# Norm sums from VectorE, one tile for the beta and decay weights, real-token queries, regrouped tail additions

## The chip, the cores and the metric

The kernel runs on one core of a Trainium2 chip. Its engines run side by side: TensorE (PE in the rows; PEld is its weight load), VectorE (DVE), ScalarE (ACT), GpSimd (POOL) and SyncE (SP), whose queue starts the DMA transfers. The metric is the device time of one execution in microseconds (us), lower is better. The kernel before takes 1480.57 us (median of three runs, 1480.06 to 1481.06).

## The reference

Two transformer blocks, one after the other, on 512 tokens of width 1024, in float32. Cut to what the change touches:

```
def second_block(x, meta_tokens, w_in, ...):                 # after first_block
    h = concatenate([meta, x], axis=1)                       # 16 meta tokens + 512 real ones = 528
    u = rms_norm(h, norm_mix_pre)                            # norm 2 of the kernel: sum of squares over 1024
    proj = u @ w_in                                          # dq dk dv dz | db da | aq ak av
    beta = sigmoid(db); g = -exp(a_log) * softplus(da + dt_bias)     # 8 + 8 columns of w_in
    o_dn = gated_deltanet(dq, dk, dv) ; o_dn = rms_norm(o_dn) * silu(dz)
    q, k = rope(rms_norm(aq)), rope(rms_norm(ak))            # heads of 64
    o_at = softmax(q k^T) v
    h = h + rms_norm(concat(o_dn, o_at) @ w_out, norm_mix_post)      # norm 3
    u = rms_norm(h, norm_mlp_pre)                            # norm 4
    h = h + rms_norm(square(relu(u @ w_up)) @ w_down, norm_mlp_post) # norm 5, the last
    return h[:, 16:]                                         # the real tokens alone
```

The output leaves the meta tokens out, so the second block needs queries (`aq`) and the gate `dz` for real tokens only; keys, values and the recurrence need all 528. Norm 0 and norm 1 are those of the first block, whose SiLU feed-forward part ends right before norm 2.

## The kernel before, in words

Activations lie transposed: features on the 128 partitions, tokens along the row, so a width of 1024 is 8 tiles of 128 x 512 (or 528). Weights come as a stream of 204 units of 128 x 1024 (512 KB each). SyncE loads a unit into one of two `raw` buffers, GpSimd splits it into `w_hi` and `w_lo` (L467, L472) in one of four slots, and TensorE multiplies three products per tile of inner dimension (hi x hi, hi x lo, lo x hi): 24 matmuls of 512 columns for one unit. Where all 528 tokens are wanted, they are done in two halves of 264, 48 matmuls per unit. Semaphores order everything; each engine runs its own list in the order written. A split needs its slot free (`unit_done`) and its buffer loaded (`raw_ready`).

Units around the change: 88 to 109 are the down projection of the first block (the last two, 108 and 109, in `down_last`, tile by tile of the output, `f_done` after each), 110 and 111 keys and values (`tile_pair`, L1051), 112 to 115 the attention queries (`wide`, L1032), 116 to 131 the four parts of the recurrence (`wide_part`, L1374; the last four, `d` from 12, are `dz`), 132 to 139 the output projection, 140 to 203 the last feed-forward part.

A norm over features needs, for each token, the sum of squares over its 1024 values. ScalarE squares each of the 8 tiles into two alternating buffers (`n_sq`). Norms 0, 1, 3 and 4: VectorE adds the tiles into `n_rs` (`add_squares`, L1901) and one matmul with a matrix of ones sums over partitions (`sum_all`, L1078). Norms 2 and 5: a matmul with ones for each tile (`squares`, L1072), accumulating in PSUM; in norm 5 these stand between the tiles of `down_last`. These matmuls have float32 operands, and each shows as two rows. ScalarE then makes the inverse root with Ln and Exp (`root`), VectorE scales (`parts`: L1656 and L1642, both hi and lo of the next input).

The beta and decay columns (16 of them) are multiplied as three padded products of 128 columns (L1298), stored by ScalarE as rows (`bat`) and turned by five transposes (L1308).

For each tile of keys or queries the normal work is: ScalarE takes the squares and the scaled values out of PSUM (`k2_in`), a matmul sums over each head (`k2_side`, L1290), ScalarE makes the root (`k2_root`), VectorE rotates (L2030 to L2041).

The tail: VectorE scales the 8 tiles of the last norm (L2334) and adds the odd ones to `xT` (L2339), GpSimd adds the even ones (L546), SyncE writes each of the 8 tiles out (L445).

Of the kernel before, what the change touches and what calls it, by code (L numbers as in the profile page):

```python
# [139 lines left out]
def build(nc, w_stream, w_ba, x_t, vec, cst, cst1, cst2, pos, out):  # L140
    ctx = ExitStack()
    with ctx:
# [24 lines left out]
        AC = 23700  # L167
        arena = sb("arena", [P, AC])

# [114 lines left out]
        bat = n_h[0:16, 0, :]  # L284
# [4 lines left out]
        wba_hi, wba_lo = (g[:].rearrange("p a b -> p (a b)")[:, 0:KT * P].rearrange("p (a b) -> p a b", b=P) for g in (g_hi, g_lo))  # L289
# [89 lines left out]
        SUMMED = (0, 1, 3, 4)  # L379

# [28 lines left out]
        def _(sp):  # L409
# [40 lines left out]
        def _(pool):  # L450
            def split(i, held=False):
                for j in range(4):
                    if held and j == 3:
                        pool.wait_ge(S["h_ready"], parts_before(3))
# [21 lines left out]
            split(U_UP // 4, True)  # L476
            with pool.Fori(U_UP // 4 + 1, n0, 1) as i:
                split(i)
# [65 lines left out]
            for f in range(0, KT, 2):  # L544
# [5 lines left out]
        def _(act):  # L550
# [19 lines left out]
            def root(n, src, w):  # L570

                if n in SUMMED:
                    act.wait_ge(S["sum_done"], SUMMED.index(n) + 1)
# [176 lines left out]
            for j in range(2):  # L750
                act.wait_ge(unit_done[(us + j) % 4], ring_before(us, j, 5))
                a(g_hi[:, j, :], M1[:, 20 + j, :], ACT.Copy).then_inc(S["ms_hi"], 1)

# [3 lines left out]
            act.wait_ge(S["ba_loaded"], 16)  # L757
            act.wait_ge(S["ba_split"], 1)
            a(wba_hi[:, :, 0:16], wba32, ACT.Copy).then_inc(S["ba_split"], 1)

# [11 lines left out]
            def k2_in(t, n, u, gain):  # L772
# [3 lines left out]
                if t == 1:  # L776
                    act.wait_ge(S["ba_split"], 3)
                wait(act, S["k2_dve"], t - 1)
                a(flat(sq2[t % 2]), two(n), ACT.Square)
                a(flat(val2[t % 2]), two(n), ACT.Copy, scale=gain).then_inc(S["t2_read"], 1)  # L780

            def k2_root(t):
                act.wait_ge(S["k2_side"], t + 1)
                r = flat(root2[t % 2])
                inverse_root(ps[:, 4:6, 0:HALF], r, r, 1.0 / 64, vcol("eps"), S["k2_sqrt"])
# [5 lines left out]
            a(bat.rearrange("p (a b) -> p a b", a=2), ps[0:16, 4:6, 0:HALF], ACT.Copy).then_inc(S["bat_ready"], 1)  # L791
# [43 lines left out]
            def dn_copy(d):  # L835
# [4 lines left out]
                if d >= 12:  # L840

                    a(DZ[:, d - 12, 0:HALF - META], two(0)[:, 0, META:HALF], ACT.Copy)
# [788 lines left out]
        def _(dve):  # L1631
# [262 lines left out]
            def add_squares(n, f):  # L1894

                if f == 0:
                    return
# [503 lines left out]
```

## Time and profile before

| | before |
|---|---|
| median of 3 runs | 1480.57 us |
| profiled execution, time | 1483.68 us |
| profiled execution, span of the trace | 1481.6 us |
| mean granted TensorE clock | 0.977 of full speed |
| PE busy | 1388.2 us (94%) |
| DVE busy | 733.0 us (49%) |
| ACT busy | 430.8 us (29%) |
| POOL busy | 767.3 us (52%) |

The page profile shows one execution. Busy shares are over the whole span. The "chain" is the work followed back from the last instruction, at each step to what released it, so the time on it is time that the end waited for. Matmul rows overlap (one starts before the one ahead has drained), so the distance from start to start counts, not the duration. Windows give the granted clock as a share of 2.4 GHz: 1.00 is 2.4 GHz, 0.50 is 1.2 GHz.

### The profile page before, as it was taken

To read this page: it belongs to the slowest core of one execution; us is meant where nothing else is said; L and a number is where in the kernel's file an instruction comes from. 1 tells how busy PE (TensorE), PEld (TensorE's weight loads), DVE (VectorE), ACT (ScalarE), POOL (GpSimd) and SP (SyncE) were. 2 spreads that over 40 slices of the span, in tenths; PEclk is the share of its full clock that TensorE was granted. 3 is DMA by queue.
4 is the path that set the end of the run, shared out by engine and by line. 5 is a ranking of instruction groups with operands and counts; after the bars stand their busy time and mean duration, and the time that the engine had idled before them with its cause. 6 is when DMAs were issued, how large, how long until landed. Compare 5 with 4: busy or idle time off the path is not lost.

```text
span 1481.6 us, 20335 instructions
## 1 busy us (share of the span) xinstructions
PE 1388.2 (94%) x7550; PEld 1140.1 (77%) x7550; DVE 733.0 (49%) x1113; ACT 430.8 (29%) x842; POOL 767.3 (52%) x443
## 2 busy tenths in 40 slices
PE   7899999899999999999889999859989999999996
PEld 5677777687888887887888887639767888888884
DVE  6967766725544545113678885596534111211112
ACT  4254444413112112111344444334423111111111
POOL 5444533266666666765235432305255666676661
PEclk9999999999999999999999999978999999999998
DMA  5222211123222222222121111000022232233221
GB/s 190 86 85 71 86 57 62 53 87 114 95 92 97 99 99 86 99 99 86 44 71 43 53 49 53 20 1 2 29 86 71 99 99 93 91 100 99 99 71 57
DMA packets 31740, 113.87 MB, mean 77 GB/s; under 512 B 3520, under 2 KB 3904, under 8 KB 31424
## 3 DMA queue, kind: packets, MB, share of 16 engines
q1 hardware_dynamic: 31536, 112.85, 22.9%
q8 instruction: 42, 0.69, 0.2%
q10 hardware_dynamic: 144, 0.18, 0.0%
q14 instruction: 18, 0.15, 0.0%
HBM read 110.92 MB, written 2.10 MB: 76 GB/s over the span
## 4 chain that ended last, share of the span: by engine, by line
PE 83%; DVE 9%; ACT 4%; issue 2%; POOL 1%; DMA 1%; DVEq 0%; SPq 0%; ACTq 0%; POOLq 0%
PE ps L1032 40%; PE ps L1234 18%; PE ps L1374 6%; ACT arena L554 3%; PE ps L1051 3%; PE ps L1065 2%; PE ps L1254 1%; PE ps L1348 1%; PE ps L1072 1%; PE ps L1176 1%; PE ps L1328 1%; PE ps L1165 1%; PE ps L1137 1%; DVE arena L2166 1%; DVE arena L2171 1%
## 5 line engine op out<-in xcount | busy, mean ns | idle before, releaser
L472 POOL TENSOR_TENSOR w_lo<-raw,w_hi 128x1024 fp32r<-128x1024 f32 x204 | 515.1, 2526 | 66.6 <-ACT w_hi L554 50.9
L467 POOL TENSOR_SCALAR w_hi<-raw 128x1024 fp32r<-128x1024 f32 x188 | 202.4, 1076 | 544.1 <-PE ps L1032 184.9
L1032 PE MATMUL ps<-h_hi,w_hi 128*128 128x512 f32 (+1 forms) x976 | 377.3, 392 | 8.6 <-DVE arena L1685 5.2
L1032 PE MATMUL ps<-h_lo,w_hi 128*128 128x512 f32 (+1 forms) x976 | 370.1, 384 | 0.0
L1032 PE MATMUL ps<-h_hi,w_lo 128*128 128x512 f32 (+1 forms) x976 | 369.9, 384 | 0.0
L1032 PEld LDWEIGHTS ps<-h_hi,w_hi 128*128 128x128 f32 x976 | 182.3, 189 | 55.0 <-issue 10.6
L1032 PEld LDWEIGHTS ps<-h_lo,w_hi 128*128 128x128 f32 x976 | 182.4, 189 | 37.8 <-issue 2.5
L1032 PEld LDWEIGHTS ps<-h_hi,w_lo 128*128 128x128 f32 x976 | 182.3, 189 | 36.2
L554 ACT ACTIVATE arena<-ps 128x512 f32<-128x512 f32 (+7 forms) x205 | 96.5, 505 | 272.5 <-PE ps L1032 41.9
L554 ACT ACTIVATE arena<-arena 128x512 f32<-128x512 f32 (+6 forms) x191 | 101.5, 534 | 224.4 <-DVE arena L2319 134.2
L1234 PE MATMUL ps<-g_hi,w_hi 128*128 128x512 f32 x400 | 155.7, 389 | 0.9 <-DVE arena L1932 0.9
L1234 PE MATMUL ps<-g_hi,w_lo 128*128 128x512 f32 x400 | 155.6, 389 | 0.0
L1234 PE MATMUL ps<-g_lo,w_hi 128*128 128x512 f32 x400 | 155.6, 389 | 0.0
L1943 DVE TENSOR_TENSOR g_lo<-arena,g_hi 128x512 fp32r<-128x512 f32 x54 | 47.9, 896 | 212.9 <-ACT g_hi L554 212.9
L554 ACT ACTIVATE arena<-ps,V 128x512 f32<-128x512 f32 (+1 forms) x114 | 80.6, 725 | 195.8 <-DVE ps L1927 127.0
L554 ACT ACTIVATE g_hi<-arena 128x512 fp32r (+2 forms) x55 | 33.8, 625 | 219.0 <-PE ps L1234 218.3
L2319 DVE SCALAR_TENSOR_TENSOR arena<-ps,arena 128x512 f32<-128x512 f32 x32 | 21.8, 690 | 135.2 <-PE ps L1032 128.7
L1234 PEld LDWEIGHTS ps<-g_hi,w_hi 128*128 128x128 f32 x400 | 75.1, 188 | 17.0 <-DVE arena L1932 1.4
L1234 PEld LDWEIGHTS ps<-g_hi,w_lo 128*128 128x128 f32 x400 | 75.1, 188 | 15.6
L1234 PEld LDWEIGHTS ps<-g_lo,w_hi 128*128 128x128 f32 x400 | 75.1, 188 | 15.4
L2073 DVE SCALAR_TENSOR_TENSOR arena<-arena,V 128x528 f32<-128x528 f32 x48 | 62.3, 1298 | 18.1 <-ACT arena L554 16.8
L1927 DVE TENSOR_TENSOR ps<-ps,arena 128x512 f32<-128x512 f32 x33 | 23.1, 699 | 89.0 <-PE ps L1032 88.9
(283 smaller groups left out, 1863.5 us busy)
## 6 DMA issues: line engine op xcount, KB each, us to landing
raw<-in_w_stream SPq DMA_DIRECT2D x204, 512.0 KB, 3.5
xT<-in_x_t SPq DMA_DIRECT2D x2, 1056.0 KB, 7.2
out<-xT SPq DMA_DIRECT2D x8, 256.0 KB, 2.1
C<-in_cst SPq DMA_DIRECT2D x1, 576.0 KB, 10.1
arena<-in_cst SPq DMA_DIRECT2D x1, 528.0 KB, 4.3
arena<-in_pos SPq DMA_DIRECT2D x1, 256.0 KB, 3.9
V<-in_vec ACTq DMA_DIRECT2D x1, 174.5 KB, 5.9
band<-in_cst SPq DMA_DIRECT2D x1, 160.5 KB, 3.7
```

The lines of the kernel that those rows point to most:

```text
L467: pool.tensor_scalar(w_hi[j][:], raw[j % 2][:], 1.0, 1.0, ALU.mult, ALU.mult).then_inc(S["pool_step"], 1)
L472: pool.tensor_tensor(w_lo[j][:], raw[j % 2][:], w_hi[j][:], ALU.subtract).then_inc(split_done[j], 1)
L554: return nc.scalar.activation(o, i, f, **kw)
L1032: last = mm(dst[p], w[:, k, :], h[:, k, cols], start=(k == 0 and n == 0), stop=(k == KT - 1 and n == 2))
L1051: last = mm(dst[e][p], w[:, k, :], h[:, k, cols], start=(c == 0 and m == 0), stop=(c == KT - 1 and m == 2))
L1065: last = mm(ps[:, e, :], w[:, k, :], h[:, k, :], start=(k == 0 and m == 0), stop=(k == KT - 1 and m == 2))
L1234: last = mm(ps[:, f, :], w[:, f, :], h[:, j, :], start=(start and n == 0), stop=(stop and n == 2), skip_group_check=True)
L1374: last = mm(two(0)[c], w[u % 4][:, k, :], h[:, k, halves[c]], start=(k == 0 and n == 0), stop=(k == KT - 1 and n == 2))
L1927: v.tensor_tensor(ps[:, q + 1, :], ps[:, q + 1, :], n_ri[:, 0:T], ALU.mult).then_inc(S["up_scaled"], 1)
L1943: v.tensor_tensor(g_lo[:, j, :], src[:, ds(4 * i + j), :].rearrange("p a b -> p (a b)"), g_hi[:, j, :], ALU.subtract).then_inc(S["ms_ready ...
L2073: ins = v.scalar_tensor_tensor(out=y5, in0=x5[:, d % 2, j:j + L], scalar=vcol("dconv", 12 * j + d), in1=y5, op0=ALU.mult, op1=ALU.add)
L2319: v.scalar_tensor_tensor(out=rb[:, q, :], in0=ps[:, q, :], scalar=0.0, in1=n_ri[:, 0:T], op0=ALU.max, op1=ALU.mult).then_inc(S["relu_ready ...
```

## The change

- **Squares.** `squares` is gone. Every norm but the first is now summed in the same way: VectorE adds the squares of tiles 0 to 6 into `n_rs`, and `sum_all` multiplies ones with `n_rs` (waits for the seventh tile's addition) and then ones with the last square itself (waits for ScalarE alone), accumulating. Norm 2 has 4 such matmuls of 264 columns in place of 16, norm 5 two of 512 in place of eight and none between the tiles of `down_last`; norms 1, 3 and 4 have two of 512 in place of one, and one VectorE addition less. For norm 3 ScalarE squares the last tile before it copies it.
- **Around norm 2.** The preparation of masks and of the beta and decay weights stands ahead of the residual additions on VectorE. GpSimd does not begin unit 112 before the eight parts of norm 2's result are written (`held` at unit 112, `h_ready` 32).
- **Beta and decay.** hi and lo of the weights lie side by side in one tile (columns 0 to 15 and 32 to 47), multiplied with h_hi and h_lo: 32 matmuls in place of 48. The two groups of rows are added while they are turned: five float32 matmuls with a stationary operand of 48 rows and a selecting matrix of 16 columns, in place of five transposes.
- **Real tokens.** Units 112 to 115 and 128 to 131 are 24 matmuls of 512 columns in place of 48 of 264, with the work behind them (head sums, roots, rotation, copies) on 512 columns.
- **Tail.** VectorE scales all 8 tiles first and then adds tiles 4 to 7; GpSimd adds tiles 0 to 3.

```
-        wba_hi, wba_lo = (g[:]....[:, 0:KT * P].rearrange(...) for g in (g_hi, g_lo))
+        wba = arena_r[:, FT * T:FT * T + KT * P].rearrange("p (a b) -> p a b", b=P)
+        two_rows = band[0:48, 0:16]
...
             for f in range(KT):
-                if f % 2:
-                    sp.wait_ge(S["x_ready"], 24 + f // 2 + 1)
+                if f >= 4:
+                    sp.wait_ge(S["x_ready"], 24 + f - 3)
                 else:
-                    sp.wait_ge(S["x_pool"], f // 2 + 1)
+                    sp.wait_ge(S["x_pool"], f + 1)
                 sp.dma_start(out[:, f, :], xT[:, f, REAL]).then_inc(S["out_done"], 16)
...
-            with pool.Fori(U_UP // 4 + 1, n0, 1) as i:
+            with pool.Fori(U_UP // 4 + 1, U_DN2 // 4 - 1, 1) as i:
+                split(i)
+            split(U_DN2 // 4 - 1, 0)
+            with pool.Fori(U_DN2 // 4, n0, 1) as i:
                 split(i)
...
-            def squares(n, f, dst, cols):
-                pe.wait_ge(S["sq_ready"], 8 * n + f + 1)
+            def sum_all(n, dst, cols):
+
+                pe.wait_ge(S["sq_used"], 8 * n + 7)
                 for p, c in enumerate(cols):
-                    last = mm(dst[p], ones[:], n_sq[:, f % 2, c], start=(f == 0), stop=(f == KT - 1))
+                    mm(dst[p], ones[:], n_rs[:, c], start=True, stop=False)
+                pe.wait_ge(S["sq_ready"], 8 * n + 8)
+                for p, c in enumerate(cols):
+                    last = mm(dst[p], ones[:], n_sq[:, 1, c], start=False, stop=True)
                 last.then_inc(S["sq_used"], 1)
...
-                tile(u, 0, two(n), halves)
+                tile(u, 0, [ps[:, 2 * (n % 2), :]], [REAL])
...
-                for n, (w, h) in enumerate(((wba_hi, h_hi), (wba_hi, h_lo), (wba_lo, h_hi))):
+                for n, h in enumerate((h_hi, h_lo)):
...
-                last = nc.tensor.transpose(ps[:, 2, 16 * b:16 * b + 16], bat[:, c0:c0 + P], cst_ap("ident")[0:16, 0:16])
+                last = mm(ps[:, 2, 16 * b:16 * b + 16], bat[:, c0:c0 + P], two_rows, start=True, stop=True)
...
+            for n, name in enumerate(("ident", "neg_f", "neg_b")):
+                last = v.tensor_copy(masks[:, n, :], cst_ap(name))
+            last.then_inc(S["masks_ready"], 1)
+
+            dve.wait_ge(S["ba_loaded"], 16)
+            v.tensor_scalar(wba, cst_ap("ident").unsqueeze(1).to_broadcast([P, KT, P]), 0.0, None, ALU.mult).then_inc(S["ba_split"], 1)
             for f in range(KT):
                 dve.wait_ge(S["f_done"], f + 1)
                 v.tensor_tensor(xT[:, f, REAL], xT[:, f, REAL], ps[:, f, :], ALU.add).then_inc(S["x_ready"], 1)
...
+                if f:
+                    add_squares(2, f - 1, L)
...
             for f in range(KT):
                 scaled(f)
-                if f % 2:
-                    added(f)
+            for f in range(4, KT):
+                added(f)
```

How the order on the engines changes at three places. VectorE at the end of the first block, before (`f_done` rows are the residual additions):

```order
L1943 TENSOR_TENSOR g_lo<-arena,g_hi 128x512 [waits ms_hi] x2
L1960 TENSOR_TENSOR xT<-xT,ps 128x512 [waits f_done] x8
L1962 CAST masks<-C 128x128 x3
L1965 TENSOR_SCALAR g_hi<-C 128x1024
L1966 TENSOR_SCALAR g_lo<-C 128x1024
L1969 TENSOR_TENSOR g_lo<-arena,g_hi 128x8x16 [waits ba_split]
L1656 SCALAR_TENSOR_TENSOR arena<-xT,V,arena 128x528 [waits rs_ready]
```

and in the changed kernel, where L1903 adds squares and L1970 the residual:

```order
L1944 TENSOR_TENSOR g_lo<-arena,g_hi 128x512 [waits ms_hi] x2
L1960 CAST masks<-C 128x128 x3
L1964 TENSOR_SCALAR arena_r<-C 128x1024 [waits ba_loaded]
L1965 TENSOR_TENSOR band<-C 48x16
L1967 TENSOR_TENSOR arena_r<-arena,arena_r 128x8x16 [waits ba_split]
L1970 TENSOR_TENSOR xT<-xT,ps 128x512 [waits f_done] x3
L1903 TENSOR_TENSOR arena<-arena 128x528 [waits sq_ready]
L1970 TENSOR_TENSOR xT<-xT,ps 128x512 [waits f_done]
L1903 TENSOR_TENSOR arena<-arena 128x528 [waits sq_used,sq_ready]
L1970 TENSOR_TENSOR xT<-xT,ps 128x512 [waits f_done]
...
L1658 SCALAR_TENSOR_TENSOR arena<-xT,V,arena 128x528 [waits rs_ready]
```

The preparation moved ahead of the residual additions, one of the two 128x1024 fills is gone, and six additions of squares stand between and behind the residual additions. TensorE at the last matmuls of the program, before:

```order
L1254 MATMUL ps<-g_hi,w_lo 128x512
L1072 MATMUL ps<-arena,ones 128x512 [waits sq_ready]
L1072 MATMUL ps<-arena,ones 128x512 [waits f_done,sq_ready]
L1072 MATMUL ps<-arena,ones 128x512 [waits sq_ready] x2
L142 UNCONDITIONAL_BRANCH
```

and now:

```order
L1264 MATMUL ps<-g_hi,w_lo 128x512
L1084 MATMUL ps<-arena,ones 128x512 [waits f_done,sq_used,f2_ready]
L1087 MATMUL ps<-arena,ones 128x512 [waits sq_ready]
L142 UNCONDITIONAL_BRANCH
```

Behind the last product stand two matmuls with ones in place of four, and the four that stood further up between the tiles are gone too. VectorE in the tail, before:

```order
L2329 COPY arena<-ps 128x512 [waits sq_ready]
L2334 SCALAR_TENSOR_TENSOR arena<-arena,V 128x512 [waits rs_ready,f2_ready]
L2334 SCALAR_TENSOR_TENSOR arena<-ps,V,arena 128x512
L2339 TENSOR_TENSOR xT<-xT,arena 128x512 [waits f2_ready]
L2334 SCALAR_TENSOR_TENSOR arena<-ps,V,arena 128x512 x2
L2339 TENSOR_TENSOR xT<-xT,arena 128x512 [waits f2_ready]
```

and now:

```order
L2333 COPY arena<-ps 128x512 [waits sq_ready]
L1903 TENSOR_TENSOR arena<-arena 128x512 [waits sq_ready]
L1903 TENSOR_TENSOR arena<-arena 128x512 [waits sq_used,sq_ready] x5
L2340 SCALAR_TENSOR_TENSOR arena<-arena,V 128x512 [waits rs_ready,f2_ready]
L2340 SCALAR_TENSOR_TENSOR arena<-ps,V,arena 128x512 x7
L2345 TENSOR_TENSOR xT<-xT,arena 128x512 [waits f2_ready] x4
```

The additions to `xT` no longer stand between the scalings, and the additions of the squares stand ahead of them.

## Rows read from the trace of the kernel before

**Rows 1.** The page, chain that ended last, shares by engine.
```profile
PE 83%; DVE 9%; ACT 4%; issue 2%; POOL 1%; DMA 1%; DVEq 0%; SPq 0%; ACTq 0%; POOLq 0%
```
**Rows 2.** Chain in order of time, around norm 2: start us, us, what.
```profile
696.50 7.89 PE ps L1072 x32
...
704.41 0.71 ACT arena L554
...
708.15 13.44 PE ps L1051 x96
721.59 5.87 PE ps L1298 x48
...
729.36 0.41 PE ps L1308 x5
...
736.73 5.86 PE ps L1032 x48
```
**Rows 3.** Timeline of VectorE, end of the first block: start us, us, engine, line, work.
```profile
696.23 0.69 DVE L1960 TENSOR_TENSOR xT<-xT,ps 128x512 f32<-128x512 f32 x1 [0.67 <-PE ps L1254]
696.84 3.53 DVE L1962 CAST masks<-C 128x128 fp32r<-128x128 f32 x3
```
**Rows 4.** Windows of 1 us: length, PE, PEld, DVE, ACT, POOL busy (x), clock, DMA.
```profile
709.00:710.00 1.00, 1.00 (x8) 1.00 (x7) 0.96 (x2) 0.49 (x1) 0.00 (x0) 0.58 0.00 0
...
712.00:713.00 1.00, 1.00 (x8) 1.00 (x7) 0.96 (x3) 0.33 (x1) 0.00 (x0) 0.71 0.00 0
...
1108.00:1109.00 1.00, 1.00 (x5) 0.73 (x4) 1.00 (x3) 0.72 (x1) 0.00 (x0) 0.74 0.00 0
```
**Rows 5.** Chain at norm 1, norm 3 and norm 4.
```profile
345.89 0.86 PE ps L1078 x2
...
1096.87 1.09 ACT arena L554 x2
...
1097.99 0.70 DVE arena L1901
...
1098.73 1.14 PE ps L1078 x2
...
1104.96 23.71 PE ps L1065 x96
1128.67 0.88 PE ps L1078 x2
```
**Rows 6.** Timeline of TensorE: four float32 matmuls of 16 columns or so.
```profile
756.85 0.52 PE L1385 MATMUL ps<-arena,C 128*128 128x16 f32 x4
757.22 0.39 PE L1386 MATMUL ps<-arena,ones 128*128 128x32 f32 x2
```
**Rows 7.** Chain among the query tiles.
```profile
751.41 2.22 DVE arena L2031
...
757.91 2.80 DVE arena L2033
```
**Rows 8.** Timeline of GpSimd, same stretch.
```profile
757.41 2.72 POOL L472 TENSOR_TENSOR w_lo<-raw,w_hi 128x1024 fp32r<-128x1024 f32 x1
```
**Rows 9.** Chain, one of the `dz` units.
```profile
902.14 6.07 PE ps L1374 x48
```
**Rows 10.** Chain, last feed-forward part and last norm.
```profile
1449.19 5.45 PE ps L1254 x24
...
1463.63 3.61 PE ps L1072 x8
```
**Rows 11.** Timeline of the tail, ScalarE, VectorE and GpSimd.
```profile
1467.26 0.69 ACT L554 ACTIVATE arena<-ps,V 128x512 f32<-128x512 f32 x1 [1.22 <-PE ps L1072]
...
1468.72 0.75 DVE L2334 SCALAR_TENSOR_TENSOR arena<-arena,V 128x512 f32<-128x512 f32 x1 [16.82 <-ACT arena L554]
...
1471.29 1.40 DVE L2334 SCALAR_TENSOR_TENSOR arena<-ps,V,arena 128x512 f32<-128x512 f32 x2
...
1477.83 1.20 DVE L2339 TENSOR_TENSOR xT<-xT,arena 128x512 f32<-128x512 f32 x1
...
1469.56 1.26 POOL L546 TENSOR_TENSOR xT<-xT,arena 128x512 f32<-128x512 f32 x1 [27.25 <-DVE arena L2334]
```

More of the change, by code:

```diff
@@ L167, in build @@
         AC = 23700
+        with nc.sbuf_tensor("arena_r", [P, AC], F32R) as arena_r:
+            pass
         arena = sb("arena", [P, AC])
@@ L450, in _, with split @@
         def _(pool):
-            def split(i, held=False):
+            def split(i, held=None):
                 for j in range(4):
-                    if held and j == 3:
-                        pool.wait_ge(S["h_ready"], parts_before(3))
+                    if held == j:
+                        pool.wait_ge(S["h_ready"], parts_before(3) if j == 3 else parts_before(4))
                     pool.wait_ge(raw_ready[j % 2], 16 * (2 * i + j // 2 + 1))
@@ L543, in _ @@
                 split(i)
-            for f in range(0, KT, 2):
+            for f in range(4):
                 pool.wait_ge(S["f2_ready"], f + 2)
@@ L1243, in down4, with down_last @@
                 return body
-            def down_last(u0, j0, n, beside=None):
+            def down_last(u0, j0, n):
                 for e in range(2):
@@ L1267, in _ @@
             pe.wait_ge(S["x_ready"], 10)
-            for f in range(KT):
-                squares(2, f, [ps[:, 0, 0:HALF], ps[:, 1, 0:HALF]], halves)
+            sum_all(2, [ps[:, 0, 0:HALF], ps[:, 1, 0:HALF]], halves)
             pe.wait_ge(S["rs_ready"], 3)
@@ L1372, in wide_part @@
                     for n, (w, h) in enumerate(((w_hi, h_hi), (w_hi, h_lo), (w_lo, h_hi))):
-                        for c in range(2):
-                            last = mm(two(0)[c], w[u % 4][:, k, :], h[:, k, halves[c]], start=(k == 0 and n == 0),
-                                      stop=(k == KT - 1 and n == 2))
+                        for c, part in enumerate(halves if d < 12 else (REAL,)):
+                            last = mm(two(0)[c] if d < 12 else ps[:, 0, :], w[u % 4][:, k, :], h[:, k, part],
+                                      start=(k == 0 and n == 0), stop=(k == KT - 1 and n == 2))
                 if ks.stop == KT:
@@ L1617, in _ @@
                 down(U_DOWN2, FT, FT2 // 4 - 1, j, False, False)
-            def sum_beside(f):
-                if f == 3:
-                    pe.wait_ge(S["f2_ready"], 1)
-                if f >= 3:
-                    squares(5, f - 3, [ps[:, 0, :]], ALL)
-            down_last(U_DOWN2 + FT2 - 2, 2, FT + FT2, sum_beside)
-            for f in range(KT - 3, KT):
-                squares(5, f, [ps[:, 0, :]], ALL)
+            down_last(U_DOWN2 + FT2 - 2, 2, FT + FT2)
+            pe.wait_ge(S["f2_ready"], 1)
+            sum_all(5, [ps[:, 0, :]], ALL)
         @block.vector
```

94 lines of the change are left out of this document (46 added, 48 removed).

## Prediction

> **What bounds the kernel now.** I read the page first. The chain that ended last is TensorE for 83% of the span and VectorE for 9% [rows 1], so an edit counts where it takes matmuls out of TensorE's list or shortens a stretch in which TensorE waits. Then I read the chain in order of time at the six places that the change touches. At norm 1 and norm 4 it runs through the matmul with ones (0.86 and 0.88 us) [rows 5]. At norm 2 it runs through 7.89 us of matmuls with ones, then ScalarE's root, then the next pair of units, the beta and decay products, the five transposes and the query units [rows 2]. At norm 3 it goes ScalarE, VectorE's addition, the matmul, the root [rows 5]. The `dz` units are in it [rows 9], and so are the last norm and the tail [rows 10, 11]. All six are on the path; none lies behind a slack engine. The sum below is made against the profiled execution (1483.68 us, span 1481.6); the median shown is 3.1 us under it, and I take the same difference off both, since nothing here works on launch or end.
>
> **Norm 1 and norm 4: +1.7.** Each gets a second matmul with ones, behind the first, on the path. From start to start one is 0.86 us [rows 5]. The VectorE addition that goes was done long before TensorE arrived in both. 2 x 0.86 = +1.7. If the addition had been late the cost would be less, so the bounds are +1.0 and +1.8.
>
> **Norm 2: -4.9, and +0.4 for the clock.** The eighth residual addition starts at 696.23 and the next instruction of VectorE at 696.84 [rows 3]. In its place stands the addition of the seventh square, 0.70 us for one such addition [rows 5]; so `n_rs` is ready at about 697.6. The 32 rows of 7.89 us are 0.247 us each [rows 2]; four matmuls are 8 rows, 1.95 us. The last square (0.6 to 0.7 us for a ScalarE instruction of this width [rows 11], behind the residual addition that ends at 696.92) is ready before the second pair starts. The root then starts near 699.5 in place of 704.41 [rows 2]: -4.9. VectorE must keep pace in `down_last`: a tile takes 5.45/4 = 1.36 us [rows 10], a residual addition and an addition of squares take 0.61 + 0.70 = 1.31 as started back to back. It just fits, provided GpSimd is quiet; with GpSimd held before unit 112 it is, from about 689 on. Without that cover the casts show the price: 3.53 us for three small ones [rows 3] while GpSimd splits. The preparation that moved ahead has the 10.5 us in which VectorE now waits for the first finished tile; at the price seen (3.5 for the casts, about 3 for one fill) it ends some 3 us before that.
>
> The clock takes a little back. Before, TensorE worked until 704.4, waited until 708.15 and was granted 2.4 GHz until a little past 709, then 1.2 GHz until past 712 (0.58 and 0.71 in the mixed windows) [rows 4]: about 3.1 us at half clock, in a unit pair that TensorE bounds (13.44 us for 96 rows, where 48 pairs at 0.245 would be 11.7). Now TensorE idles sooner, from 696.2 with only 2 us of work in it, so the low clock is there from the first instruction, as it was behind norm 3, where work began at 1104.96 [rows 5] and 2.4 GHz came back in the window from 1108 (0.74) [rows 4], 3.5 us later or a little more. 0.5 to 0.8 us more at half speed costs 0.3 to 0.4.
>
> **Beta and decay: -1.4.** 48 matmuls in 5.87 us [rows 2] become 32: -1.95. Five transposes in 0.41 us [rows 2] become five float32 matmuls, two rows each. Four rows of such size take 757.22 - 756.85 = 0.37 [rows 6], so ten take 0.93: +0.5. Bounds +0.3 and +1.5, the upper if each row were as long as one with 264 columns divided by two.
>
> **Queries: -1.7.** A unit of 48 matmuls takes 5.86 us [rows 2], one of 24 matmuls of 512 columns 5.45 [rows 10]: -0.42 for a unit, four units. The first two are followed on the path by TensorE, and count in full. Behind the third the path runs through VectorE's rotation (2.22 and 2.80 us for instructions that take 0.7 alone) [rows 7]. These end when GpSimd's subtraction ends: the one of 2.72 us from 757.41 to 760.13 [rows 8] lies over the 2.80 us that end at 760.71. GpSimd starts when TensorE frees the slot, so it comes earlier by the same 0.42 and 0.84, and VectorE with it. So the last two count too, and I take -1.7; were they lost it would be -0.85, and with the narrower instructions on VectorE at most -2.1. The page "SBUF — State Buffer" of the Trainium skill, section "Who interferes with whom", says that a VectorE instruction with two SBUF inputs and a GpSimd instruction that reads SBUF exclude each other for the whole instruction; by that the third and fourth unit count in full, and rows 7 and 8 agree.
>
> What could spoil it is the hold. Units 112 and 113 are now split after norm 2's parts, from about 712.8, and with 114 and 115 GpSimd is busy without a break for 14 us, over the first rotation. TensorE wants unit 112 near 723, some 7 us after it is ready, and the rotated keys near 729, one or two us after I expect them. I cost it at nothing; if the cover fails, +1 to +3.
>
> **`dz` units: -1.75.** Same exchange, 6.07 us with the start [rows 9] less 0.42, four times, all on the path: -1.7, and one copy on ScalarE in place of two, -0.05. Bounds -1.0 and -2.1.
>
> **Norm 3: -1.0.** Before: two ScalarE instructions (1.09), the addition (0.70), the matmul, whose start to the root is 1.14 [rows 5]; the root starts 3.05 us after the last product. Now the matmul on `n_rs` starts at once (0.86), ScalarE squares first (0.60), and the second matmul ends 0.86 + 1.16 = 2.0 after the product: -1.0, bounds -0.8 and -1.3.
>
> **Norm 5: -4.95.** The last 48 products start at 1449.19 and take 2 x 5.45 = 10.9 [rows 10] without the four sums between them, so the last tile is finished at 1460.3. The seventh square (ready 1.36 before) is squared and added by 1460.2, so the two matmuls run at once: 0.86 + 1.16, root at 1462.3. Before it starts at 1467.26 [rows 11]. Bounds -4.2 and -5.1.
>
> **Tail: -1.8.** Before, from the first scaling at 1468.72 to the end of the last addition at 1479.03 is 10.3 us [rows 11]: 8 scalings at 0.68 and four additions of 1.20 that wait for GpSimd's 1.26. Now 8 scalings in 5.4 (they read PSUM and ran at 0.70 each beside GpSimd [rows 11]). GpSimd's four additions start 0.85 after the first and end 5.2 later, at 6.05; VectorE's first addition ends 0.55 behind that, three more take 0.63 each: 8.5. The output transfers follow 0.63 us apart; after the last one 2.6 us pass to the end of the span, as now. Bounds -0.9 (the transfers queue up) and -2.3.
>
> **Sum.** 1.7 - 4.9 + 0.4 - 1.4 - 1.7 - 1.75 - 1.0 - 4.95 - 1.8 = -15.4. Profiled execution 1468.3, median 1480.57 - 15.4 = **1465.2**.
>
> **Rivals.**
> - Two narrow matmuls cost only their share of columns. A pair of 264 costs 5.86/24 = 0.244 us and one of 512 costs 5.45/24 = 0.227 [rows 2, 10]; the gain of both groups of units, 3.4 us, rests on that 0.017, and the two figures come from different loops. If the pair cost 0.227 x 528/512 = 0.234 by itself and the rest were the loop's, 192 pairs would give 192 x 0.007 = 1.4 in place of 3.4: 1467.2. Against it: whole units, in the same run, at the same clock. Chance 0.1. "TensorE: Matmul & The Clock Gate" of the Trainium skill, section "Back-to-back issue gap", has a rule that leans the same way, N/2.4 + 2.5 ns from start to start: 225 ns for the pair, 216 for the wide one, an estimated 1.8 us for all. By that rule the sum would be -13.8; the rows are above it in both forms (244 and 227), more so in the narrow one.
> - Contention takes more: GpSimd's four splits in a row over the first rotation, or VectorE falling behind its 1.36 us for a tile in `down_last`. Place: 686 to 735. +2 to +5, time 1467 to 1470. For it: 2.22, 2.80 and 3.53 us for short instructions. Against: the hold covers norm 2, and the rotation has slack. Chance 0.17.
> - Slower than before: the hold starves TensorE. If after the hold each unit's split waited for its own load and for VectorE, and TensorE came to units 112 to 115 with none of them ready, four waits of 5 us or more would be needed to eat 15.4. The point is a split ready later than 723 + 5.45 per unit; GpSimd's larger half of a unit takes 2.72 us [rows 8], the whole some 3.5 to 4, and two raw buffers are full when the hold ends. Time 1482. Chance 0.02.
> - Norm 5 and the tail give less because ScalarE, VectorE and TensorE pass the last squares more slowly or the eight transfers bunch: -4.5 in place of -6.75, time 1467.4. Chance 0.1.
> - The forecast itself, within 1463.2 to 1467: 0.61.
>
> **How the numbers follow.** The forecast's own bounds, most ends taken at half, make 1463 to 1467. The contention case reaches to 1470; below, the clock or VectorE's overlap could give back 2 more. Range 1462.0 to 1469.5. A change of 0.2% is 3.0 us, about what a measurement tells from none. All cases but the third lie beyond it: faster 0.97, within 0.2% 0.015, slower 0.015.
>
> **What would show it.** Root of norm 2 about 3.5 us after the last residual addition begins (now 8.2); the unit pair behind it at low clock from its first row; 32 rows with the new weight tile near 3.9 us; query units 5.45 from start to start; norm 3's root 2.0 after its last product; norm 1 and 4 with two rows pairs of 0.86; last product to last root 2.0; first scaling to last addition 8.5. I am wrong if TensorE waits for `w_hi` at unit 112 or later, if residual additions in `down_last` drift behind `f_done`, or if VectorE's rotations are longer than before by more than 2 us in sum.

## The result, and the profile after

The changed kernel takes 1471.18 us in the median (1470.23 to 1473.29, 4 runs), the kernel before beside it 1480.82: ratio 0.9924, interval 0.9909 to 0.9939. It is 9.6 us faster; 15.4 were forecast, and 1471.18 lies outside the range.

Both profiled executions carry a part that has nothing to do with the change: no instruction differs ahead of the sum of norm 1, and yet the pair of units right ahead of that sum starts at 334.73 us before and at 331.57 after. Over all 17 profiles of this study that start lies between 331.57 and 338.22. So from here on I measure from the start of this pair, "from norm 1" for short, to the end of the span: 1481.60 - 334.73 = 1146.87 before, 1468.10 - 331.57 = 1136.53 after, a gain of 10.3 us.

The chain in order of time around norm 2 and the beta and decay products, after (start us, us, what), which answers [rows 2]:

```profile
694.51 0.71 DVE arena L1903
695.36 1.13 PE ps L1084 x4
696.49 0.90 PE ps L1087 x4
697.42 0.71 ACT arena L558
...
701.16 13.45 PE ps L1057 x96
714.61 3.92 PE ps L1306 x32
718.56 0.61 ACT arena L558
719.31 1.13 PE ps L1298 x4
720.44 1.21 PE ps L1316 x10
```

The 7.89 us of sums are 2.03 (L1084, L1087), behind the addition of the seventh square (0.71). The root (697.42) starts 3.5 us after the last product's end at 693.88, in place of 8.2. The pair of units is as long as before: 13.45 against 13.44, so the 0.4 that I gave the clock here did not fall due. The 48 beta products of 5.87 us are 32 of 3.92, but the ten rows that took the place of five transposes cost 1.21.

The chain at norm 3 and in the tail, after, which answers [rows 5, 10, 11]:

```profile
1089.93 0.86 PE ps L1084 x2
1090.79 0.97 PE ps L1087 x2
1091.78 0.70 ACT arena L558
...
1453.79 1.10 PE ps L1084 x2
1454.88 0.87 PE ps L1087 x2
1455.78 0.70 ACT arena L558
1456.50 0.64 ACT arena L558
1457.24 5.36 DVE arena L2340 x8
1462.60 0.95 DVE xT L2345
1463.56 0.60 DVEq L142
1464.16 1.21 DVE xT L2345 x2
```

The last norm runs two matmuls behind the last product, and eight scalings take 5.36 us before VectorE's additions: both as forecast.

What was not forecast shows in the windows. Columns are length, then PE, PEld, DVE, ACT and POOL busy (x instructions), granted clock (1.00 is 2.4 GHz, 0.50 is 1.2 GHz), DMA share, GB/s. The changed kernel at the start of the attention loop, at the first decay products, and late in the recurrence:

```profile
760.40:767.00 6.60, 5.21 (x24) 5.25 (x25) 5.08 (x9) 0.86 (x4) 0.95 (x1) 0.50 0.26 82
934.40:937.80 3.40, 3.40 (x7) 1.67 (x6) 0.00 (x0) 0.60 (x1) 2.49 (x5) 0.51 0.00 0
996.00:1002.50 6.50, 4.83 (x89) 4.64 (x89) 1.83 (x5) 2.15 (x5) 4.49 (x4) 0.50 0.01 3
```

The kernel before at the same two places, attention and first decay products:

```profile
770.60:774.00 3.40, 3.40 (x16) 3.40 (x17) 3.26 (x7) 0.77 (x2) 0.00 (x0) 0.50 0.43 159
943.22:947.00 3.78, 3.78 (x20) 2.73 (x21) 0.00 (x0) 1.20 (x2) 3.67 (x7) 1.00 0.02 4
```

At the attention loop half clock fills all 6.6 us of the window, which begins 1.4 us ahead of the loop (761.78 us), in place of 3.4 us from the loop's start (770.58). And it stands at the decay products, where in this execution of before it did not.

### The profile page after: what moved, and what is told of

Read it like the earlier page. It is cut to its first block, busy times and chain, and to the rows that moved or that the text cites. A ratio compares the mean times of both kernels' runs of the same rounds, so it can differ in the third digit from the quotient of the medians.

```text
span 1468.1 us, 19860 instructions
## 1 busy us (share of the span) xinstructions
PE 1373.4 (94%) x7309; PEld 1119.2 (76%) x7309; DVE 736.6 (50%) x1122; ACT 430.6 (29%) x838; POOL 768.2 (52%) x443
## 4 chain that ended last, share of the span: by engine, by line
PE 83%; DVE 10%; ACT 4%; issue 2%; POOL 1%; DMA 1%; DVEq 0%; SPq 0%; ACTq 0%; POOLq 0%
PE ps L1038 41%; PE ps L1244 18%; PE ps L1382 6%; ACT arena L558 3%; PE ps L1057 3%; PE ps L1071 2%; PE ps L1264 1%; DVE arena L2077 1%; PE ps L1356 1%; PE ps L1186 1%; PE ps L1336 1%; PE ps L1175 1%; PE ps L1147 1%; DVE arena L2175 1%; DVE arena L2170 1%
## 5 line engine op out<-in xcount | busy, mean ns | idle before, releaser
L1038 PE MATMUL ps<-h_hi,w_hi 128*128 128x512 f32 x944 | 376.4, 399 | 7.1 <-DVE arena L1687 4.3
L1038 PE MATMUL ps<-h_lo,w_hi 128*128 128x512 f32 x944 | 369.5, 391 | 0.0
L1038 PE MATMUL ps<-h_hi,w_lo 128*128 128x512 f32 x944 | 369.2, 391 | 0.0
L1038 PEld LDWEIGHTS ps<-h_hi,w_hi 128*128 128x128 f32 x944 | 178.2, 189 | 54.1 <-issue 10.4
L1038 PEld LDWEIGHTS ps<-h_lo,w_hi 128*128 128x128 f32 x944 | 178.1, 189 | 39.3 <-issue 2.9
L1038 PEld LDWEIGHTS ps<-h_hi,w_lo 128*128 128x128 f32 x944 | 178.3, 189 | 37.7
L558 ACT ACTIVATE arena<-ps 128x512 f32<-128x512 f32 (+6 forms) x201 | 96.4, 512 | 267.4 <-PE ps L1038 37.7
L558 ACT ACTIVATE g_hi<-arena 128x512 fp32r (+1 forms) x54 | 33.5, 630 | 218.3 <-PE ps L1244 218.3
L1244 PEld LDWEIGHTS ps<-g_hi,w_lo 128*128 128x128 f32 x400 | 75.1, 188 | 15.4
```

The costliest lines, as they stand in the source:

```text
L558: return nc.scalar.activation(o, i, f, **kw)
L1038: last = mm(dst[p], w[:, k, :], h[:, k, cols], start=(k == 0 and n == 0), stop=(k == KT - 1 and n == 2))
L1244: last = mm(ps[:, f, :], w[:, f, :], h[:, j, :], start=(start and n == 0), stop=(stop and n == 2), skip_group_check=True)
```

## The experiments

All stages below are read between the same instructions in each chain of waits: from their starts, or from the end of what released them. Each ratio is to the kernel before run in the same round. Its medians lay between 1480.82 and 1483.62 us, so kernels of different rounds are compared by their ratios. The first four kernels asked whether the missing time is clock or size.

**ctl_before and ctl_after**, both kernels unchanged.

> The kernel before, unchanged, for a second profile of it. Both theories expect 1480 to 1481 us. What it tells apart: in the first profile the stretch up to the first norm's last column took 3.16 us longer than in the profile of the changed kernel, though no instruction there differs. If that belongs to one execution, the second profile has this stretch 2 to 3 us shorter and the rest (norm 1 to the end) again at 1146.9 within 1 us; if it belongs to the kernel, it stays.

> The changed kernel, unchanged, for a second profile of it. Both theories expect 1470 to 1473 us. Theory A (the missing 4 to 5 us are lost where TensorE's clock is granted at half, and these stretches moved with the change: start of attention +0.8, start of the decay stage +1.7, recurrence +0.9): the second profile shows the low stretches at the same places of the program, the one at the start of the decay stage above all. Theory B (the terms of the queries, of the second wide stage and of the small fp32 matmuls were too large, and the low clock is scatter between executions): the low stretches lie elsewhere in this profile, and the time of the profiled execution moves by 1 to 3 us with them, while the stage of the queries gains 0.7 us again and not 1.7.

Medians 1482.99 (ratio to before 1.0005, 0.9993 to 1.0016) and 1471.78 (0.9921, 0.9901 to 0.9942). From norm 1 to the end the second profile of before has 1146.99 (1480.30 - 333.31), that of after 1136.76 (1470.20 - 333.44), within 0.12 and 0.23 of the first ones. So these executions differ ahead of norm 1, by up to 2 us, and their sums behind it agree; theory B's scatter of 1 to 3 us is not in them. But my sharpest piece of evidence moved: the second profile of before has half clock at the decay products too.

```profile
943.00:947.00 4.00, 4.00 (x16) 3.00 (x15) 0.00 (x0) 1.19 (x2) 2.86 (x5) 0.57 0.02 4
```

These products then take 1.7 us longer, and 1.4 of it came back later: from the first decay product to the end of the recurrence the two profiles of before have 105.54 and 105.85, the two of after 108.06 and 108.23. The stretch of decay and recurrence as a whole is 2.4 longer after, not its first products alone.

**one_sum**: norms 1 and 4 as before.

```
-                            sum_all(1, [ps[:, 7, :]], ALL)
+                            sum_one(1)
...
-                    sum_all(4, [ps[:, 7, :]], ALL)
+                    sum_one(4)
...
-                if f == 0 or f == KT - 1:
+                if f == 0 or (f == KT - 1 and n not in (1, 4)):
```

> The changed kernel with norms 1 and 4 as before: VectorE adds the last square and TensorE sums columns with one matmul, in place of two with the last square apart. The prediction's term for both is +1.7 us, and the two profiles agree at +0.86 each: so 1469.4 us, 1.7 below the changed kernel, by theory B. By theory A the saving can be lost or doubled by where the low stretches then fall: 1468 to 1471.

Median 1472.29 (ratio 0.9933, 0.9911 to 0.9954), no difference from the changed kernel that can be told. In the profile both terms are there: 368.75 against 369.59 between norms 1 and 2, 27.33 against 28.19 at norm 4. Then the pair behind norm 2 took 14.26 in place of 13.45:

```profile
700.48 14.26 PE ps L1057 x96
```

Half clock there lasted 6.8 us in this kernel and 3.4 in the changed one, and of the 1.7 us 1.0 is left from norm 1 to the end (1135.57 against 1136.53). That the shortening brought the 0.8 us at this pair is not shown: in narrow_z below, whose instructions up to here are those of the changed kernel, the pair took 14.42.

**keep_clock**: matmuls in TensorE's waits.

```
+            def fill(bank, w, x, count):
+                for _ in range(count):
+                    mm(ps[:, bank, :], w, x, start=True, stop=True)
...
+            fill_w(U_AT2, 5, 14)
...
+            fill(6, h_hi[:, 0, 0:P], h_hi[:, 1, 0:T], 14)
...
+            fill(6, h_hi[:, 0, 0:P], h_hi[:, 1, 0:T], 8)
...
+            fill_w(U_UP2, 5, 18)
...
+                    fill(6, h_hi5[:, 0, 0:P], h_hi5[:, 1, :], 8)
```

In this order they stand behind the sum of norm 2, ahead of the attention loop, behind its last sums, behind the sum of norm 3 and behind that of norm 4; `fill_w` waits for the unit's weights and calls `fill`.

> The changed kernel with filler matmuls of 128 by 512, whose results nobody reads, in five of TensorE's waits: 14 behind the sum of norm 2, 14 ahead of the loop of attention, 8 behind the last sum of the recurrence's norm, 18 behind the sum of norm 3, and 8 behind the sum of norm 4. Theory A: the granted clock stays at 1 across these waits, the wide stages behind them lose their slow first 3.4 to 6.8 us, and the kernel gains 3 to 7 us over the changed one (1464 to 1468). Theory B: filler does not reach the terms that were mis-sized; each filler that lasts longer than its wait costs what it sticks out (0.23 us a matmul), so 1471 to 1474.

Median 1463.26 (1461.14 to 1465.8), ratio 0.9867 (0.9841 to 0.9892): some 8 us below the changed kernel, a little more than the 3 to 7 of theory A. From norm 1 to the end 1127.85, 8.7 less. In its chain the pair behind norm 2 lasts 11.90:

```profile
703.74 11.90 PE ps L1057 x96
```

Its windows at the starts of that pair, of the attention loop and of the decay products have the full clock:

```profile
703.74:707.00 3.26, 3.26 (x27) 3.26 (x28) 3.19 (x5) 1.30 (x2) 0.00 (x0) 1.00 0.00 0
762.70:766.00 3.30, 3.28 (x27) 3.28 (x28) 3.12 (x8) 0.77 (x2) 0.00 (x0) 1.00 0.54 159
932.50:936.00 3.50, 3.49 (x17) 2.46 (x18) 0.00 (x0) 1.19 (x2) 3.38 (x7) 1.00 0.00 0
```

So half clock behind TensorE's waits costs this kernel 8.7 us, and it can be bought off with work that nobody reads. That alone doesn't say that it ate the change's gain; the same filler in the kernel before does.

**keep_before**: the kernel before with the same five lines.

> The kernel before with the same filler matmuls in the same five waits (their results are read by nobody). Filler took 8.6 us off the changed kernel, from the start of norm 1 to the end. Theory A (part of the gain that the prediction promised went into low-clock time that moved or grew: 0.8 at the start of attention, 2.35 in decay and recurrence, 0.5 at norms 3 and 4): filler takes less off the kernel before, 4 to 6 us, because it has less such time in these places, and changed minus before, both with filler, comes near -14. Theory B (the terms were mis-sized and the clock is the same burden on both): filler takes 8 to 9 off this one too, and the difference with filler stays at -10.3.

Median 1477.33, ratio 0.9954 (0.9937 to 0.9971). From norm 1 to the end 1141.42: filler takes 5.5 us off, not 8.7, as theory A had it. By stage (us; two profiles of before, two of after, then both with filler):

| stage | before | after | with filler | work | clock |
|---|---|---|---|---|---|
| pair at norm 1 to pair at norm 2 | 373.42, 373.41 | 369.59, 369.57 | 373.45, 369.59 | -3.86 | 0 |
| pair at norm 2 | 13.44, 13.45 | 13.45, 13.44 | 11.90, 11.90 | 0 | 0 |
| beta and decay | 8.18, 8.18 | 7.04, 7.03 | 8.18, 7.04 | -1.14 | 0 |
| two query units | 12.85, 12.87 | 12.27, 12.24 | 12.87, 12.24 | -0.63 | 0 |
| up to the attention loop | 27.96, 27.90 | 27.86, 27.86 | 27.88, 27.80 | -0.08 | 0 |
| attention loop | 172.64, 172.65 | 172.00, 172.08 | 171.09, 169.79 | -1.30 | +0.7 |
| decay and recurrence | 105.54, 105.85 | 108.06, 108.23 | 106.47, 106.94 | +0.47 | +2.0 |
| output units, norm 3 | 56.06, 56.05 | 55.04, 55.04 | 56.06, 55.10 | -0.96 | 0 |
| units behind norm 3, norm 4 | 26.82, 26.70 | 28.19, 28.21 | 25.17, 26.00 | +0.83 | +0.6 |
| last feed-forward, norm 5 | 335.60, 335.59 | 330.68, 330.70 | 333.99, 329.09 | -4.90 | 0 |
| tail | 14.36, 14.34 | 12.35, 12.36 | 14.36, 12.36 | -2.00 | 0 |
| sum | 1146.87, 1146.99 | 1136.53, 1136.76 | 1141.42, 1127.85 | -13.6 | +3.3 |

"Work" is the difference of the two kernels with filler, "clock" what the difference without filler adds to it (means of two).

At the attention loop and behind norm 3 filler took time off both kernels, 0.7 and 0.6 us more off the changed one. In all six profiles of kernels that start the loop as the changed one does, without filler, half clock there lasts 6.8 us; in all three that start it as the kernel before does (tail_only is the third), 3.4. In decay and recurrence it is otherwise: filler took 1.2 off the changed kernel (108.15 to 106.94) and added 0.8 to the kernel before (105.70 to 106.47). So "clock" in that row is a difference in where half clock fell, not a price that filler took off.

**tail_only**: the kernel before with norm 5's squares on VectorE and the new tail.

```
-            down_last(U_DOWN2 + FT2 - 2, 2, FT + FT2, sum_beside)
-            for f in range(KT - 3, KT):
-                squares(5, f, [ps[:, 0, :]], ALL)
+            down_last(U_DOWN2 + FT2 - 2, 2, FT + FT2)
+            pe.wait_ge(S["f2_ready"], 1)
+            sum_two(5, ps[:, 0, :])
...
```

> The kernel before with only the last norm's squares summed on VectorE and the tail regrouped. The prediction's terms -4.95 and -1.8: 6.75 below the kernel before, and every stage ahead of the last 48 products as before within 0.1 us, the low-clock stretches too. If the two terms had lived on something else in the change they would come out at under 5.

Median 1474.27, ratio 0.9940 (0.9917 to 0.9963). The two stages are 330.67 and 12.37, to 0.03 as in the changed kernel: 6.9 off, alone. These edits stand behind every other stage, so there is no later clock to answer. The rest of the kernel together was then worth 10.3 - 6.9 = 3.4 us, where 8.65 were forecast.

**narrow_q**, the changed kernel with the query units on 528 columns in halves again, and **keep_nq** and **full_nq**, the same with filler.

```
-                tile(u, 0, [ps[:, 2 * (n % 2), :]], [REAL])
+                tile(u, 0, two(n), halves)
...
```

> The changed kernel with units 112 to 115 on all 528 columns in halves, as before. Prediction's term: +1.7 (0.42 a unit, all four on the path). What the profiles suggest instead: 0.28 a unit for the two units that TensorE bounds, and nothing for the third and fourth, whose time lies under VectorE's rotation: +0.6 up to the start of the attention loop. The low-clock stretch at the start of the loop may then change as well: with it 0 to +1.5 in all. If the two last units count, it is +1.1 or more at that point.

> The kernel with the five fillers (results read by nobody) and units 112 to 115 on 528 columns in halves again. Without filler, undoing the queries' edit cost 0.63 us where the units run, and 0.95 came back in the recurrence, so that from norm 1 to the end nothing was left (1136.46 against 1136.53). Theory A (what came back is clock, not work): with the clock held the edit keeps its 0.6 to 0.7: from norm 1 to the end 1128.5 against 1127.85 without this undoing. If it is not clock, the difference is again near 0.

Medians 1468.11 (ratio 0.9890, 0.9871 to 0.9910) and 1464.22 (0.9858, 0.9829 to 0.9888). The two units that TensorE bounds take 12.87 in place of 12.24, each time; from there to the attention loop 27.90 and 27.87 against 27.86 and 27.80. So the edit is worth 0.6 where it stands, not 1.7. In the changed kernel's chain the path leaves TensorE behind the second unit:

```profile
733.92 1.76 ACT arena L558 x3
...
736.35 1.28 ACT L558
...
742.62 2.04 DVE arena L2035
...
749.40 2.41 PE ps L1382 x18
```

It runs through ScalarE and VectorE and comes back to TensorE at other products; the third and fourth unit are not on it. And the 0.6 did not survive: from norm 1 to the end narrow_q has 1136.46, the changed kernel 1136.53 and 1136.76. I expected it to survive with the filler; it did not either (1127.28 with the edit undone, 1127.85 with it). The recurrence's second part, which begins with VectorE's copy behind the decay products, takes 89.75 us in keep_nq and 90.80 in keep_clock and took it back, though its instructions are the same. The ratio of narrow_q, 0.9890, even lies below the changed kernel's 0.9921 (the intervals overlap), where 0.6 us more were expected. Its profile is of the longest of its four executions and doesn't show why; this stays open.

**keep_rec, best, full_before, full_after**: filler in the recurrence, where the windows of keep_clock still have the clock at 0.53 for 32 us:

```profile
968.00:1000.00 32.00, 17.82 (x448) 15.83 (x450) 25.73 (x54) 6.12 (x14) 10.14 (x10) 0.53 0.01 2
```

```
-            pe.wait_ge(S["b_act"], 9)
+            pe.wait_ge(S["b_act"], 12)
+            fill(3, ones[:], ones[:].unsqueeze(1).to_broadcast([P, 4, P]), 4)
...
-            pe.wait_ge(S["b_act"], 12)
+            fill(3, ones[:], ones[:].unsqueeze(1).to_broadcast([P, 4, P]), 10)
```

> The changed kernel with the filler of the five waits, and 12 + 15 more matmuls with the tile of ones (128 by 512, results read by nobody) in the two waits of TensorE inside the recurrence, where the clock is low for 27 us. Theory A: the small matmuls behind them (3.1 and 2.7 us for 64 and 61 rows) and what follows run at the full clock: 2 to 3.5 us below the kernel with the five fillers only. If the stage is bounded by VectorE's substitution, and the clock does not matter there, 0; the filler that sticks out of the wait would cost up to 2.

Median 1468.93, ratio 0.9910 (0.9888 to 0.9932): slower than keep_clock. I had taken a matmul with the float32 ones for 0.23 us; it is two rows of 0.43, and the filler stood on the path for 10.57 and 13.07 us. Behind it the first level products ran faster: 5.67 us from the first of them to the 64 products of 64 x 64, where keep_clock has 8.23 to the same products. Those 64 took 2.59 + 0.94 against 3.61, for there half clock was back:

```profile
1000.50:1003.50 3.00, 2.62 (x51) 2.43 (x49) 0.19 (x1) 1.43 (x4) 3.00 (x3) 0.50 0.02 5
```

The 63 behind them took 1.90 against 2.79. From the first level product to the mark at the recurrence's end, keep_rec has 1044.15 - 994.58 = 49.57 and keep_clock 1039.45 - 986.73 = 52.72. So the low clock is worth 3.1 us there, if it can be lifted for nothing.

> The changed kernel with norms 1 and 4 as in the kernel before, the five fillers, and filler with the tile of ones (128 by 512, each two rows; results read by nobody) in the recurrence in the right size: 4 ahead of the first substitution's products, 13 ahead of the level products (27 before, which stuck out of the waits by 8 us, while the work behind them was 3.15 us shorter). Theory A: from norm 1 to the end 1127.85 - 1.7 - 3.1 = 1123 us, and the time 1458 to 1460. If the clock does not set the recurrence's second half, 1126.

It has norms 1 and 4 as before, and 4 + 13 fillers. Median 1462.86 (1460.28 to 1464.21), not 1458 to 1460; ratio 0.9856 (0.9827 to 0.9884). Faster than keep_rec; its lead over keep_clock, keep_nq (0.9858) and full_after (0.9858) is within the noise of the medians and shows in the profile alone. From norm 1 to the end it has 1124.48, the least of all, and not 1123: both norms gave their 0.8, and now kept it, since the pair behind norm 2 stays at 11.89; the recurrence's filler still sticks out, by some 2.5 us.

> The kernel before with the five fillers and, in the recurrence, 4 + 10 filler matmuls with the tile of ones (two rows of 128 by 512 each; all results read by nobody). Theory A: from norm 1 to the end 1141.4 - 3.3 = 1138 us, the recurrence's second half at the full clock.

> The changed kernel with the same fillers. Theory A: 1127.85 - 3.8 = 1124.0 from norm 1 to the end, and 14.0 us below the kernel before with the same fillers: the change's work without its clock (the forecast's terms, without its 0.4 for the clock, are 15.8). If the remaining shortfall were clock as well, the difference would be 15 to 16; if filler only shifts time about, 10 to 12.

> The same with units 112 to 115 on 528 columns in halves again. Theory A: 0.6 to 0.7 us above full_after from norm 1 to the end. If the queries' edit is worth nothing even then, 0, and its gain must be lost on the path elsewhere, in the recurrence's work and not in its clock.

Medians 1477.22 (ratio 0.9959, 0.9942 to 0.9977), 1463.19 (0.9858, 0.9839 to 0.9878) and 1464.38 (0.9862, 0.9840 to 0.9885). From norm 1 to the end 1141.24, 1127.69 and 1129.21. Here my expectation of 1138 and 1124 failed: with 4 + 10 the recurrence gains next to nothing, 0.2 to 0.3 us. The clock falls again 4.3 us behind the filler, at 993.7, among products of 32 rows with waits between them; and in full_after the first level product starts 1.6 us later than in keep_clock, which takes back most of the 1.8 gained behind it. The changed kernel with this filler:

```profile
977.72 11.66 PE ps L1095 x20
989.39 1.28 PE ps L1518 x98
...
992.84 2.23 issue
...
996.28 3.61 PE ps L1542 x64
```

The difference of before and after is 13.55, a second measure of the 13.6. And the queries' edit is worth 1.5 here, after 0 without filler and -0.6 with five: the recurrence's second part takes 90.57 in full_after and 91.59 in full_nq, whose instructions there are the same. That stage scatters by more than this edit is worth.

**no_hold**: `split(U_DN2 // 4 - 1, 0)` back to `split(U_DN2 // 4 - 1)`, so that GpSimd isn't held.

> The changed kernel without GpSimd's hold ahead of unit 112. The prediction let the gain at norm 2 (4.9) rest on this hold, since VectorE has 1.36 us for a tile and needs 1.31, and gave 3.53 us for three casts beside GpSimd as the price of no cover. If so, the stage from norm 1 to the pair behind norm 2 grows from 369.6 us by 0.5 to 3, and the residual additions drift. If the cover does nothing it stays at 369.6.

Median 1475.78, ratio 0.9938 (0.9914 to 0.9962), some 2 us over the changed kernel by the ratio; from norm 1 to the end 1138.77, 2.1 more. Between norms 1 and 2 it has 371.51 in place of 369.59. The chain of this kernel shows the place, one scaling of VectorE that takes 0.78 in the changed one; GpSimd works on a unit beside it, from 702.47 to 704.81:

```profile
701.37 0.71 ACT arena L558
...
702.78 2.60 DVE arena L1658
...
706.94 1.22 PE ps L1057 x4
```

The price comes behind the root and not in the squares that I had in mind: the sum still starts 0.95 behind the seventh square's addition (0.85 with the hold). The pair behind is 14.07, another 0.6. I put that down to TensorE's longer wait, but narrow_z has 14.42 without one, so it is not shown.

**narrow_z**: the four dz units in halves again.

```
-                        for c, part in enumerate(halves if d < 12 else (REAL,)):
+                        for c, part in enumerate(halves):
...
```

> The changed kernel with the four dz units in halves again. Prediction's term: +1.75. The profiles say 0.34 an iteration: the loop of attention grows by 1.36 us (172.0 to 173.4). The clock behind it is as before or shifts by up to 1 us either way.

Median 1472.81, ratio 0.9916 (0.9884 to 0.9948), the same as the changed kernel. The attention loop has 173.39 in place of 172.04, so +1.35. Two units of narrow_z and of the changed kernel, from start to start 11.61 and 11.26, first narrow_z:

```profile
897.04 6.08 PE ps L1383 x48
908.65 6.07 PE ps L1383 x48
```

```profile
893.66 5.79 PE ps L1382 x24
904.92 5.80 PE ps L1382 x24
```

From norm 1 to the end it is 1137.24, so 0.6 of the 1.35 is left: decay and recurrence together took 106.16 in place of 108.15, the pair behind norm 2 14.42 in place of 13.45.

```profile
703.20 14.42 PE ps L1058 x96
```

The pair stands ahead of this edit. Up to it narrow_z and the changed kernel have the same instructions and the same time from norm 1 (369.54 and 369.59), and still half clock lasts 6.8 us in one and 3.4 in the other. So at this place its length differs between executions, whatever the edit.

**The recurrence over all profiles.** From the first decay product to the first level product takes 54.2 us where the decay products have the full clock (before, full_before and all kernels with the five fillers alone), 55.9 where half clock lies on them for 3.4 us (the second profile of before, tail_only, both of after, one_sum, narrow_q, no_hold), and 57.2 in narrow_z, with 6.9 us of it. From the first level product to the recurrence's end it is 48.6 to 50.0 us in the five profiles with at most 3.6 us of half clock there (the second of before, tail_only, narrow_z, keep_rec, best) and 50.9 to 53.3 in the twelve with 6.8 to 13.7. Windows that begin 3.7 to 6.1 us behind the first level product, in the two profiles of before, then in the changed kernel and in narrow_z:

```profile
1001.50:1009.00 7.50, 6.85 (x188) 6.62 (x189) 4.03 (x7) 3.04 (x7) 6.22 (x6) 0.50 0.02 4
1001.50:1009.00 7.50, 4.94 (x218) 4.79 (x219) 4.78 (x8) 3.77 (x9) 6.48 (x6) 1.00 0.02 4
995.80:1002.60 6.80, 5.12 (x97) 4.94 (x95) 2.03 (x5) 2.33 (x6) 4.49 (x4) 0.50 0.01 2
999.00:1006.00 7.00, 5.28 (x215) 5.01 (x214) 5.12 (x8) 4.00 (x9) 6.23 (x6) 1.00 0.02 5
```

So without filler each profile of before pays at one of the two places, and the changed kernel, one_sum, narrow_q and no_hold pay at both. What decides where half clock falls is not shown.

## Why the prediction was wrong

The direction and the places were right, and the edits at the end came out to 0.2 us. Measured from norm 1, the gain is 10.3 us and so 5.1 short. With filler in both kernels 13.6 of the forecast's 15.8 without its clock term are there; this leaves 2.2 for sizes, 0.5 of it in the recurrence, which I had at nothing and which scatters by more. The clock took 3.3 where I had put 0.4; this is the other 2.9.

- **The step that failed is the clock's.** I priced it at one place, +0.4 behind norm 2, and left it at nothing everywhere else, though the trace of before had half clock behind norm 3 [rows 4]. It cost +0.7 at the attention loop, +0.6 behind norm 3 and +2.0 in decay and recurrence. For the first and the second filler shows that it is clock, and every profile repeats them. For the recurrence it is shown in part: its length follows the half clock that falls in it, over all 17 profiles, and filler inside it brought its last part from 52.7 to 48.6 and 49.6 us. But of the 2.0 only 1.2 is what filler took off the changed kernel, and narrow_z, with the changed kernel's instructions there, is just 0.5 us over the kernel before. Why the low stretches fall where they do stays open.
- **The one place that I priced.** Behind norm 2 the two profiled kernels have 13.44 and 13.45, so 0. That is the chance of these executions: the six profiles with the new norm 2 and no filler lie between 13.43 and 14.42, with a mean of 13.85, the three with the old one between 13.44 and 13.46.
- **Queries, -1.7: was -0.7.** Two faults. A unit saved 0.28 and not 0.42: I took the new form's 5.45 from another loop, where in this one it is 5.57, which is the first rival's point (worked out there as 2.0 less for both groups). And I counted the third and fourth unit, which are behind ScalarE and VectorE: that VectorE's rotation waits for GpSimd did not carry their saving to the path, for up to the attention loop it is 27.96 and 27.86.
- **dz units, -1.75: was -1.3.** The same 0.28 a unit, 5.79 for 6.07, and 0.35 an iteration.
- **Beta and decay, -1.4: was -1.14.** -1.95 as worked out, but the ten rows cost 1.21 for 0.41, so +0.8 where I took +0.5; it lay within the bounds.
- **Norm 2, -4.9: was -4.7.** -3.86 less norm 1's +0.86. **Norms 1 and 4, +1.7:** 0.82 to 0.86 each in one_sum and best. **Norm 3, -1.0:** -0.96 to -1.02. **Norm 5, -4.95:** -4.90. **Tail, -1.8:** -2.0.
- **The rivals.** That narrow matmuls cost only their share held in part, with 8 units of 0.14, 1.1 us. Contention did not come: the hold works, and no_hold shows what it is worth, 1.9 us up to the pair behind norm 2. The starving of TensorE at unit 112 did not come either.
- **The range** gave each size its bounds and the clock none above its 0.4. The result lies 1.7 us above its end; the 0.7, 2.4 and 0.6 of the three places come to 3.7.

## What to carry to other kernels

Where TensorE waits and then works at half clock, an edit that shortens the work ahead may not be worth its microseconds: the low stretch can fall on more of the work behind, as it did at the attention loop. Price each such place with both signs, or take the edits that stand behind the last of them, which came out to 0.2 us here. Compare profiles by stages that begin at the same instruction: but for one shift of 1.7 us the stages agreed to 0.3 us between the two profiles of each kernel, while single times of it lay 2 to 6 apart. Take more than two where half clock is near: the pair behind norm 2 differed by 1.0 and the recurrence by 2 us between profiles with the same instructions. And fill the waits ahead of wide stages: five groups of matmuls that nobody reads gave 8.7 us here, beside 10.3 for the whole change.

## What the hardware showed that I had not expected

- The granted clock falls at the same places of the program in both profiled executions of the changed kernel; of the kernel before, one execution had none at the decay products and one had. It need not last as long: behind norm 2 it was 3.4 us in the changed kernel and 6.8 in narrow_z, with the same instructions up to there.
- Filler doesn't hold it for long among small products: in full_after half clock was back 4.3 us behind the end of 11.66 us of filler, amid products of 32 rows and waits of up to 2.23 us, and the next 64 products took 3.61 us as without filler. Whether the products or the waits brought it back is not told apart.
- A unit of 24 matmuls of 512 columns takes 5.45 us in the last feed-forward part and 5.57 to 5.80 among the query and `dz` units, at the same granted clock.
- A VectorE scaling of 0.78 us takes 2.60 while GpSimd splits a unit, as the rotations did (2.22 and 2.80) [rows 7].
